# Early weight halves on VectorE, operand sums in a PSUM bank, a new order of memory attention: a two-block transformer forward pass on one core

## The chip, the cores and the metric

The kernel runs on one core of a Trainium2 chip. The metric is device time in microseconds of one execution, the median of several. The kernel before takes 3501.17 us (median of 3 runs, 3498.74 to 3503.02). Everything is float32; products are made on TensorE from two halves of each operand (below).

## What is computed

Two blocks are applied to x (512 tokens, width 1024). The first has two layers; each adds a mixer (layer 0: pooling and a gated recurrence, layer 1: banded attention), an attention over 256 memory tokens and a squared-ReLU MLP, with a norm ahead of and behind each:

```python
mem_n = rmsnorm(mem, mem_norm_gain)
for l in range(DEPTH):                     # 2 layers
    g = norm_gains[l]
    h = rmsnorm(x, g[0])
    y = even_mixer(h, ...) if l % 2 == 0 else odd_mixer(h, ...)
    x = x + rmsnorm(y, g[1])
    h = rmsnorm(x, g[2])
    x = x + rmsnorm(memory_cross_attention(h, mem_n, w_mem_q[l], w_mem_kv[l], w_mem_o[l]), g[3])
    h = rmsnorm(x, g[4])
    x = x + rmsnorm(squared_relu_mlp(h, w_ff1[l], w_ff2[l]), g[5])

def memory_cross_attention(h, mem_n, w_q, w_kv, w_o):      # 4 heads of 256
    q = (h @ w_q).reshape(B_, S_, MEM_HEADS, MEM_HEAD_DIM)
    kv = (mem_n @ w_kv).reshape(B_, M, 2, MEM_HEADS, MEM_HEAD_DIM)
    s = jnp.einsum('bshd,bmhd->bhsm', q, kv[:, :, 0]) * MEM_HEAD_DIM ** -0.5
    p = jax.nn.softmax(s, axis=-1)
    return jnp.einsum('bhsm,bmhd->bshd', p, kv[:, :, 1]).reshape(B_, S_, D_MODEL) @ w_o
```

The second block (a convolution and RWKV-7 mixer, then a product-key expert layer with 16384 experts) takes the rest of the time, from about 1700 us on. The change leaves its code alone.

## The kernel before, in words

**Program and queues.** Each engine has its own program, written by hand in one order: pe_program, dve_program, act_program, pool_program, sp_program. Engines meet through semaphores only (`wait_ge(at(...))`); an instruction that waits holds up everything behind it on its engine. The stages follow each other: memory (keys and values of both layers), even mixer, mem0, mlp0, odd mixer, mem1, mlp1, then the second block.

**Weights and halves.** Weights come in chunks of 1 MB through three raw buffers (`sp_loads`; the load of chunk r waits until both units of chunk r-3 are split). A chunk is two units of 128 x 1024 words. Each unit is split in two fp32r halves: ScalarE rounds it to the high half (`act_split`, L454), GpSimd subtracts to get the low half (`pool_split`, L462). The split tiles hold four units (slot u % 4), so unit u can be split only when the product that used unit u - 4 has ended (`unit_free`). A product is three matmuls per 128 rows of the contraction (`triple`, L476 to L478: high x high, low x high or high x low). Units are split AHEAD = 3 ahead of the product that reads them.

**Memory stage.** x and mem lie transposed (features on partitions, eight tiles c). ScalarE makes the high half of mem times gain (`act_operand`, L586) and its square (L587), VectorE the low half (`dve_operand_low`, L591) and the sum of the squares (`dve_operand_sum`, L598). TensorE sums them over partitions against a constant matrix (`pe_operand_sum`, L557), ScalarE takes the root (`act_root`, L572, L575), and the products are scaled by it as they leave PSUM. Keys: eight products per layer of 24 matmuls with 256 columns, one unit each (`pe_first` interleaves the first three over the eight tiles, `pe_product` makes the rest). Values: per layer four chunks, each read twice (`pe_token_product`, two token tiles tk), so a chunk's two units must both be ready at its start and come free only at its end; ScalarE scales the result (L822) between the splits of two units. Results go to DRAM by DMAs that GpSimd issues (`pool_key_out`, `pool_value_out`), three products late (KEY_LAG) so that they stand behind the splits, from rings of four buffers. The operand halves and squares of x for the even mixer are made in the same stage.

**Seams.** Between two branches (five places: even to mem0, mem0 to mlp0, mlp0 to odd, odd to mem1, mem1 to mlp1) `dve_add` on VectorE scales y by gain and root (L641), adds it to x (L648) and makes the low half (L591) of each of eight tiles; `act_add` on ScalarE first splits unit first + 3 of the next weights, then makes the high halves and squares. After the eight tiles VectorE adds the squares in y[:, 0, :] (L598, seven adds), while TensorE runs the first four products of the next stage (`pe_first` on three, then one more), and only then `pe_operand_sum`.

**Memory attention (mem0, mem1).** The order is the list of `mem_slots()`: each slot may hold a piece, which is one of the eight q products (24 matmuls with 512 columns) or a step of the first three o products, and an item m of 16 (head, token tile). TensorE does in a slot the piece, the score of item m, the transposes of item m - 3 (`pe_mem_spread`, L1373) and, where a head ended at item m - 5, its output products (`pe_mem_out`). VectorE scales q (L1450), makes its low half (L1454), the row extremes (L1464) and the normalised probabilities (L1470, L1472), and the low halves of the turned probabilities (L1495) and outputs (L1501). ScalarE makes the high halves and exponentials. Keys and values of the layer are split in halves at q piece 2 and 4 (`act_mem_halves`, `dve_mem_halves`, L1487).

PSUM has eight banks in one ring (`banks.take`, `banks.give`).

Of the kernel before, what the change touches and what calls it, by code (L numbers as in the profile page):

```python
# [9 lines left out]
F32 = mybir.dt.float32  # L10
# [4 lines left out]
P = 128  # L15
T = 512
D = 1024
CT = D // P
TT = T // P
M = 256  # L20
# [37 lines left out]
AHEAD = 3  # L58
# [198 lines left out]
def build(nc, dram, out, gate_table, early_table, memory_k, memory_v, x_tokens):  # L257
    ctx = ExitStack()
    with ctx:
# [154 lines left out]

        def split_ready(u):
            return at("split_high", u), at("split_low", u)
# [40 lines left out]
        def pool_split(upto):  # L457
            while state["low"] <= upto:
# [5 lines left out]
                state["low"] += 1  # L464

# [127 lines left out]

        def dve_operand_sum(stage, square):

            for c in range(1, CT):
                dve.wait_ge(at("operand_square", stage, c), at("operand_square", stage, 0) if c == 1 else dve.last)
                dve.do.tensor_tensor(square(0), square(0), square(c), ALU.add  # L598
                                     ).then_inc(*dve.sig("operand_sum", stage, c))
# [30 lines left out]
        def act_add(branch, stage, gain, first):  # L630
            act_split(first + AHEAD)
            for c in range(CT):
                act_operand(stage, c, x[:, c, :], gain, h_hi[:, c, :], y[:, c, :], x_ready(branch)(c))

        def dve_add(branch, gain, x_before, y_ready, stage=None, next_gain=None):
# [14 lines left out]
            if stage:  # L650
                dve_operand_sum(stage, lambda c: y[:, c, :])
# [93 lines left out]
        constant_names = ["columns"] + [k for k in CONSTANT_WIDTHS if k not in STAGE_CONSTANTS]  # L745
# [4 lines left out]
        def pool_inputs():  # L750
            for k in constant_names:
                pool.do.dma_start(columns if k == "columns" else const[k], dram[k]
                                  ).then_inc(*pool.land("constants_landed", k))
# [3 lines left out]
        def dve_inputs():  # L757
            dve.wait_ge(at("constants_landed", constant_names[-1]))
            for i, value in enumerate((NORM_EPS, LN_EPS, GN_EPS, 1.0)):
                dve.do.memset(scalars[:, i:i + 1], value).then_inc(*dve.sig("eps_set", i))  # L760
            dve_mod_gate()
# [64 lines left out]
        def pool_memory():  # L826

            pool_split(2 * W["keys", 0][0] + AHEAD)
            for l in range(2):
                for c in range(CT):  # L830
                    pool_split(2 * W["keys", l][0] + c + AHEAD)
                    if c >= KEY_LAG:
                        pool_key_out(l, c - KEY_LAG)
# [2556 lines left out]
```

## Time and profile before

| | |
|---|---|
| median of 3 runs | 3501.17 us |
| the profiled execution | 3501.14 us |
| its span in the profile | 3499.9 us |
| mean granted TensorE clock | 0.967 |

In the profile PE is TensorE, DVE VectorE, ACT ScalarE, POOL GpSimd, SP the queue that issues the weight loads; PEld is the loading of TensorE's stationary operand. L462 is line 462 of the kernel. A row of instructions names the engine, the line, the tiles written and read, and in brackets the idle time ahead of it with what ended it. Matmuls overlap: their records are longer than the distance between them, which is the rate.

### The profile page before, as it was taken

To read this page: it belongs to the slowest core of one execution; us is meant where nothing else is said; L and a number is where in the kernel's file an instruction comes from. 1 tells how busy PE (TensorE), PEld (TensorE's weight loads), DVE (VectorE), ACT (ScalarE), POOL (GpSimd) and SP (SyncE) were. 2 spreads that over 40 slices of the span, in tenths; PEclk is the share of its full clock that TensorE was granted. 3 is DMA by queue.
4 is the path that set the end of the run, shared out by engine and by line. 5 is a ranking of instruction groups with operands and counts; after the bars stand their busy time and mean duration, and the time that the engine had idled before them with its cause. 6 is when DMAs were issued, how large, how long until landed. Compare 5 with 4: busy or idle time off the path is not lost.

```text
span 3499.9 us, 48015 instructions
## 1 busy us (share of the span) xinstructions
PE 3248.4 (93%) x18529; PEld 2740.7 (78%) x18529; DVE 2253.0 (64%) x3780; ACT 1358.3 (39%) x2196; POOL 1715.9 (49%) x931
## 2 busy tenths in 40 slices
PE   6997888999899888999898898999999998999997
PEld 6886677888776677888576755799999998788886
DVE  4176646555544556553566646276998995888888
ACT  4444434222344434222253314333333674333332
POOL 6742323444332323444242202447888544888885
PEclk9998999999999999999898899999999999999999
DMA  5520212444322212443220011338899899999995
GB/s 193 183 76 25 87 58 92 137 139 139 108 91 67 84 45 88 145 144 109 69 85 31 3 37 60 120 141 292 295 325 326 266 311 304 372 357 350 354 356 219
DMA packets 304819, 584.76 MB, mean 167 GB/s; under 512 B 13520, under 2 KB 224464, under 8 KB 287312
## 3 DMA queue, kind: packets, MB, share of 16 engines
q1 hardware_dynamic: 252512, 373.32, 31.5%
q0 software_dynamic: 42576, 153.83, 12.2%
q10 hardware_dynamic: 9504, 54.53, 4.1%
q8 instruction: 149, 2.44, 0.3%
q14 instruction: 78, 0.64, 0.1%
HBM read 522.91 MB, written 58.72 MB: 166 GB/s over the span
## 4 chain that ended last, share of the span: by engine, by line
PE 64%; POOL 13%; DVE 9%; issue 8%; ACT 3%; DMA 1%; POOLq 0%; DVEq 0%; SPq 0%; ACTq 0%
PE bank L476 14%; PE bank L478 14%; PE bank L477 14%; POOL split_low L462 9%; PE twin L476 3%; PE twin L478 3%; PE twin L477 3%; PE bank L2854 2%; PE bank L557 2%; PE bank L2279 2%; POOL rows_arena L3220 2%; DVE branch L598 1%; POOL rows_h L3220 1%; POOL rows_near L3220 1%; DVE residual L648 1%
## 5 line engine op out<-in xcount | busy, mean ns | idle before, releaser
L462 POOL TENSOR_TENSOR split_low<-weights,split_high 128x1024 fp32r<-128x1024 f32 x554 | 1363.0, 2466 | 1494.7 <-ACT split_high L454 1490.9
L476 PE MATMUL bank<-normed_high,split_high 128*128 128x512 f32 (+1 forms) x2024 | 748.0, 370 | 34.6 <-issue 25.9
L477 PE MATMUL bank<-normed_low,split_high 128*128 128x512 f32 (+1 forms) x2024 | 736.7, 364 | 0.0
L478 PE MATMUL bank<-normed_high,split_low 128*128 128x512 f32 (+1 forms) x2024 | 736.5, 364 | 0.0
L454 ACT CAST split_high<-weights 128x1024 fp32r<-128x1024 f32 x554 | 571.4, 1046 | 359.8 <-PE bank L478 202.0
L476 PEld LDWEIGHTS bank<-normed_high,split_high 128*128 128x128 f32 x2024 | 384.1, 190 | 84.2 <-issue 37.0
L477 PEld LDWEIGHTS bank<-normed_low,split_high 128*128 128x128 f32 x2024 | 384.1, 190 | 41.6 <-issue 2.7
L478 PEld LDWEIGHTS bank<-normed_high,split_low 128*128 128x128 f32 x2024 | 383.3, 189 | 41.1
L476 PE MATMUL bank<-split_high,wide_hidden_high 128*128 128x512 f32 x768 | 300.2, 391 | 12.6 <-DVE wide_hidden_low L3076 7.4
L478 PE MATMUL bank<-split_high,wide_hidden_low 128*128 128x512 f32 x768 | 299.3, 390 | 0.0
L477 PE MATMUL bank<-split_low,wide_hidden_high 128*128 128x512 f32 x768 | 299.3, 390 | 0.0
L2749 ACT ACTIVATE branch<-bank 128x384 f32<-128x384 f32 x128 | 63.0, 492 | 309.0 <-PE bank L478 306.8
L476 PEld LDWEIGHTS bank<-split_high,wide_hidden_high 128*128 128x128 f32 x768 | 144.5, 188 | 45.9 <-issue 14.0
L1540 DVE SCALAR_TENSOR_TENSOR tmp<-weights,scalars,tmp 128x256 f32<-128x256 f32 x168 | 176.4, 1050 | 5.1
L3072 DVE TENSOR_TENSOR lates<-lates,gates 128x384 f32<-128x384 f32 x128 | 144.8, 1150 | 38.9 <-DMA gates<-gate_table 38.8
L478 PEld LDWEIGHTS bank<-split_high,wide_hidden_low 128*128 128x128 f32 x768 | 144.4, 188 | 30.1
L477 PEld LDWEIGHTS bank<-split_low,wide_hidden_high 128*128 128x128 f32 x768 | 144.6, 188 | 29.8
L2976 ACT CAST wide_hidden_high<-lates 128x384 fp32r<-128x384 f32 x128 | 65.6, 514 | 230.5 <-DVE lates L3072 166.6
L476 PE MATMUL bank<-hidden_high,split_high 128*128 128x512 f32 x384 | 150.7, 392 | 0.0
L3076 DVE TENSOR_TENSOR wide_hidden_low<-lates,wide_hidden_high 128x384 fp32r<-128x384 f32 x128 | 126.9, 991 | 36.0 <-ACT wide_hidden_high L2976 30.5
L478 PE MATMUL bank<-hidden_high,split_low 128*128 128x512 f32 x384 | 149.6, 390 | 0.0
L477 PE MATMUL bank<-hidden_low,split_high 128*128 128x512 f32 x384 | 149.4, 389 | 0.0
(636 smaller groups left out, 6265.3 us busy)
## 6 DMA issues: line engine op xcount, KB each, us to landing
weights<-in_w_ff SPq DMA_DIRECT2D x64, 1024.0 KB, 5.5
weights<-in_peer_u SPq DMA_DIRECT2D x64, 1024.0 KB, 7.4
weights<-in_peer_v SPq DMA_DIRECT2D x64, 1024.0 KB, 8.9
weights<-in_cond_w SPq DMA_DIRECT2D x24, 1024.0 KB, 5.3
early_table<-branch SPq DMA_DIRECT2D x128, 192.0 KB, 4.4
gate_table<-arena SPq DMA_DIRECT2D x12, 2048.0 KB, 9.8
lates<-early_table ACTq DMA_DIRECT2D x32, 768.0 KB, 9.6
gates<-gate_table ACTq DMA_DIRECT2D x32, 768.0 KB, 12.5
```

What stands on the lines that cost most here:

```text
L454: act.do.copy(unit_tiles(u)[0], raw_unit(u)).then_inc(*act.sig("split_high", u))
L462: pool.do.tensor_tensor(lo, raw_unit(u), hi.bitcast(F32), ALU.subtract).then_inc(*pool.sig("split_low", u))
L476: pe.do.matmul(o, ah, bh, start=first, stop=False)
L477: pe.do.matmul(o, ah, bl, start=False, stop=False)
L478: return pe.do.matmul(o, al, bh, start=False, stop=last)
L557: pe.do.matmul(banks.tile("sum", norm)[:, 0:n], matrix, rhs, start=i == 0, stop=i == count - 1).then_inc(*pe.sig("summed", norm, i))
L1540: dve.do.scalar_tensor_tensor(out=total, in0=wt[:, a, :], scalar=g_act[:, CT + a:CT + a + 1], in1=total, op0=ALU.mult, op1=ALU.add).then_i ...
L2279: last = pe.do.matmul(bank, raw_tile("conv", j)[:, at_tap * P:(at_tap + 1) * P], r_pad[:, c, tap:tap + T], start=tap == 0, stop=tap == CON ...
L2854: last = pe.do.matmul(bank[:, j * P:(j + 1) * P], hot[:, 0, t, :], hot[:, 1, t, :], start=True, stop=True)
L3072: dve.do.tensor_tensor(s, s, gates[n % 2][:, :, c, :], ALU.mult).then_inc(*dve.sig("gated_hidden", n, c))
L3076: dve.do.tensor_tensor(lo[:, c - 1, :], lates[n % 2][:, c - 1, :], hi[:, c - 1, :].bitcast(F32), ALU.subtract).then_inc(*dve.sig("hidden_l ...
L3220: pool.do.indirect_dma_start(out=v_rows[k % V_RING], out_offset=None, in_=dram["peer_v_rows"], in_offset=bass.IndirectOffsetOnAxis(ap=own_ ...
```

## The change

- The low halves of the first 34 units (the memory stage's 32 and the even mixer's first two) are made by VectorE (`dve_split`) and not by GpSimd, which in the memory stage now only issues DMAs, each as soon as its product is scaled (KEY_LAG is gone).
- The start waits for the columns alone, not for all constants; ScalarE loads its table first; the sigmoid of the modulation gate moves into the even mixer. The splits of the first units stand between the first operands in another order (FIRST_UNITS), and units 4 to 6 are split ahead of the root.
- VectorE makes the x operands' low halves between the values' splits, and adds their squares during layer 1's keys.
- At the five seams the running sum of the squares stands in a PSUM bank; each add reads one tile of y from SBUF. ScalarE splits unit first + 3 after the eight operands instead of ahead of them.
- In memory attention the keys' halves are made ahead of the root, and the pieces stand at other items: q4 to q7 at items 0, 3, 8, 11 (before 0, 2, 4, 6), o steps at 12, 13, 15, 16, 19, 20 (before 10, 11, 14, 15, 18, 19).

The diff, cut to its core:

```diff
+        EARLY = 2 * W["E", "f"][0] + 2
         def split_ready(u):
-            return at("split_high", u), at("split_low", u)
+            return at("split_high", u), at("early_low" if u < EARLY else "split_low", u)
+        def dve_split(upto):
+            while state["early"] <= min(upto, EARLY - 1):
+                u = state["early"]
+                hi, lo = unit_tiles(u)
+                dve.wait_ge(at("split_high", u), unit_free(u))
+                dve.do.tensor_tensor(lo, raw_unit(u), hi.bitcast(F32), ALU.subtract
+                                     ).then_inc(*dve.sig("early_low", u))
+                state["early"] += 1
+        def dve_running_sum(stage):
+            total = running_sum(stage)
+            for c in range(1, CT):
+                ...
+                dve.do.tensor_tensor(total if c < CT - 1 else y[:, 0, :], total, y[:, c, :], ALU.add
                                      ).then_inc(*dve.sig("operand_sum", stage, c))
         def act_add(branch, stage, gain, first):
+            act_split(first + FIRST - 1)
+            for c in range(CT):
+                act_operand(stage, c, x[:, c, :], gain, h_hi[:, c, :], y[:, c, :] if c else running_sum(stage),
+                            [x_ready(branch)(c), None if c else state["sum_empty", stage]])
             act_split(first + AHEAD)
-            for c in range(CT):
-                act_operand(stage, c, x[:, c, :], gain, h_hi[:, c, :], y[:, c, :], x_ready(branch)(c))
         def act_inputs():
-            act.wait_ge(at("constants_landed", constant_names[-1]), at("eps_set", 3))
-            act_mod_gate()
+            act.do.preload_act_table_set("natural_log_exp_and_others")
+            act.wait_ge(at("columns_landed"), at("eps_set", 3))
+        FIRST_UNITS = (-1, -1, 1, 1, 2, 2, 3, 3)
         def act_memory():
             for c in range(CT):
-                act_split(first + min(1 + c // 2, FIRST))
+                act_split(first + FIRST_UNITS[c])
                 ...
-            act_split(first + FIRST + 1)
-            act_logs()
+            act_split(first + 2 * FIRST)
             act_root("mem", 0, NORM_EPS, mem_root, M)
         def mem_slots():
-            slots += [(("q", 4), 0), (None, 1), (("q", 5), 2), (None, 3), (("q", 6), 4), (None, 5), (("q", 7), 6)]
-            return slots + [(("o",) if m > 9 and m % 4 in (2, 3) else None, m)
-                            for m in range(7, len(MEM_ITEMS) + OUT_LAG)]
+            pieces = {0: ("q", 4), 3: ("q", 5), 8: ("q", 6), 11: ("q", 7)}
+            pieces.update((m, ("o",)) for m in (12, 13, 15, 16, 19, 20))
+            return [(("q", c), None) for c in range(4)] + [(pieces.get(m), m) for m in range(len(MEM_ITEMS) + OUT_LAG)]
         def act_mem(l):
             act_split(q_unit + FIRST + AHEAD)
+            act_mem_halves("k", l, m_k, mk_high)
             act_root(st, 0, NORM_EPS, root)
         def dve_mem(l, before):
+            dve_mem_halves("k", l, m_k, mk_high, mk_low)
             for piece, m in mem_slots():
```

## Rows read from the trace of the kernel before

**Rows 1.** The page: the chain that ended last, by engine.

```profile
PE 64%; POOL 13%; DVE 9%; issue 8%; ACT 3%; DMA 1%; POOLq 0%; DVEq 0%; SPq 0%; ACTq 0%
```

**Rows 2.** Stretches: length, PE, PEld, DVE, ACT, POOL busy, clock, DMA share, GB/s.

```profile
64.00:87.00 23.00, 19.78 (x164) 19.43 (x163) 17.76 (x11) 9.40 (x13) 18.29 (x14) 1.00 0.53 173
87.00:110.00 23.00, 22.02 (x182) 21.67 (x181) 2.97 (x7) 7.33 (x7) 22.90 (x15) 1.00 0.70 225
```

**Rows 3.** DMA issues to 160 us: KB, median us to landing.

```profile
arena<-in_mem SPq DMA_DIRECT2D x1, 1024.0 KB, 5.6
columns<-in_columns POOLq DMA_DIRECT2D x1, 189.5 KB, 6.2
```

**Rows 4.** Timeline of the first 45 us: start, us, what, idle before.

```profile
10.07 1.28 ACT L1524 ACT_TABLE_LOAD   x1 [10.07 <-DVE scalars L760]
14.51 0.91 POOL L755 DMA_DIRECT2D residual<-in_x  x1 [9.79 <-DMA weights<-in_w_mem_kv]
15.52 9.31 POOL L462 TENSOR_TENSOR split_low<-weights,split_high 128x1024 fp32r<-128x1024 f32 x4
22.66 0.55 PE L476 MATMUL bank<-mem_high,split_high 128*128 128x256 f32 x1 [1.33 <-POOL split_low L462]
...
43.17 0.55 PE L476 MATMUL bank<-mem_high,split_high 128*128 128x256 f32 x1 [3.87 <-POOL split_low L462]
```

**Rows 5.** Timeline in the values of layer 0, and the even mixer's first sum.

```profile
60.55 0.47 ACT L822 ACTIVATE arena<-bank,token_root 128x256 f32<-128x256 f32 x1 [0.25 <-PE bank L478]
60.92 1.03 ACT L454 CAST split_high<-weights 128x1024 fp32r<-128x1024 f32 x1
63.11 0.35 PE L476 MATMUL bank<-split_high,mem_high 128*128 128x256 f32 x1 [2.60 <-POOL split_low L462]
68.39 14.00 DVE L598 TENSOR_TENSOR branch<-branch 128x512 f32<-128x512 f32 x7
70.63 0.56 POOL L852 DMA_DIRECT2D memory_v<-arena  x1
136.36 1.02 PE L557 MATMUL bank<-branch,const_mean 128*128 128x512 f32 x2
```

**Rows 6.** Forms on VectorE to 1400 us: count, busy, mean ns.

```profile
L598 DVE TENSOR_TENSOR branch<-branch 128x512 f32<-128x512 f32 x42 | 63.6, 1515 | 3.8
L1584 DVE TENSOR_TENSOR branch<-branch,bank 128x512 f32<-128x512 f32 x42 | 27.6, 681 | 35.1 <-PE bank L478 35.0
L1487 DVE TENSOR_TENSOR mem_k_low<-arena,mem_k_high 128x1024 fp32r<-128x1024 f32 x4 | 4.7, 1221 | 0.5 <-ACT mem_k_high L1426 0.5
```

**Rows 7.** VectorE writing PSUM, whole execution: count, busy, mean ns.

```profile
L3033 DVE SCALAR_TENSOR_TENSOR twin<-rows_arena,own_z,twin 128x1024 f32<-128x1024 f32 x55 | 70.8, 1287 | 10.4 <-DMA rows_arena<-in_peer_v_rows,own_expert 6.1 <-DVE twin L3033 0.5
```

**Rows 8.** Timeline of the seam into mem0.

```profile
390.46 2.70 POOL L462 TENSOR_TENSOR split_low<-weights,split_high 128x1024 fp32r<-128x1024 f32 x1 [4.91 <-ACT split_high L454]
390.87 2.84 DVE L641 SCALAR_TENSOR_TENSOR branch<-branch,columns,tmp 128x512 f32<-128x512 f32 x1
409.79 9.48 DVE L598 TENSOR_TENSOR branch<-branch 128x512 f32<-128x512 f32 x7
412.36 2.95 ACT L454 CAST split_high<-weights 128x1024 fp32r<-128x1024 f32 x3 [2.82 <-PE bank L478]
413.50 8.00 POOL L462 TENSOR_TENSOR split_low<-weights,split_high 128x1024 fp32r<-128x1024 f32 x3 [20.34 <-ACT split_high L454]
430.76 0.55 PE L476 MATMUL bank<-mem_k_high,mem_q_high 128*128 128x256 f32 x1 [4.78 <-issue]
```

**Rows 9.** Who waited for the adds of L598, whole execution: us, times.

```profile
  PE bank L557: 9.5, 3
  PE twin L557: 0.9, 2
```

**Rows 10.** TensorE's waits in mem0, 425 to 536 us: total, times, longest.

```profile
PE bank L476 <- DVE mem_turned_low L1495: 7.1, 3, 3.5
PE twin L476 <- DVE mem_turned_low L1495: 2.2, 1, 2.2
```

**Rows 11.** TensorE in a stretch of mem0: length, busy, granted clock, DMA.

```profile
480.00:490.00 10.00, 7.78 (x33) 0.83 0.00 0
```

More of the change, by code:

```diff
@@ L592, in dve_operand_low, with dve_operand_add, pe_sum_bank, running_sum @@
                                         op1=ALU.subtract).then_inc(*dve.sig("operand_low", stage, c))
+        def dve_operand_add(stage, square, c):
+            dve.wait_ge(at("operand_square", stage, c),
+                        at("operand_square", stage, 0) if c == 1 else at("operand_sum", stage, c - 1))
+            dve.do.tensor_tensor(square(0), square(0), square(c), ALU.add
+                                 ).then_inc(*dve.sig("operand_sum", stage, c))
         def dve_operand_sum(stage, square):
             for c in range(1, CT):
[L597 to L598 removed]
+                dve_operand_add(stage, square, c)
+        def pe_sum_bank(stage):
+            state["sum_empty", stage] = banks.take("running_sum", stage)[1]
+            banks.give(("running_sum", stage), ("operand_sum", stage, CT - 1))
+        def running_sum(stage):
+            return banks.tile("running_sum", stage)
+        def dve_running_sum(stage):
+            total = running_sum(stage)
+            for c in range(1, CT):
+                dve.wait_ge(at("operand_square", stage, c),
+                            at("operand_square", stage, 0) if c == 1 else at("operand_sum", stage, c - 1))
+                dve.do.tensor_tensor(total if c < CT - 1 else y[:, 0, :], total, y[:, c, :], ALU.add
                                      ).then_inc(*dve.sig("operand_sum", stage, c))
@@ L744, in build @@
         rings += [k_out, v_out]
-        constant_names = ["columns"] + [k for k in CONSTANT_WIDTHS if k not in STAGE_CONSTANTS]
+        constant_names = [k for k in CONSTANT_WIDTHS if k not in STAGE_CONSTANTS]
         def sp_inputs():
@@ L855, in dve_memory @@
         def dve_memory():
+            first = 2 * W["keys", 0][0]
+            square = lambda e: y[:, e, :]
             for c in range(CT):
+                dve_split(first + FIRST_UNITS[c])
                 dve_operand_low("mem", c, mem_raw[:, c, :], mem_gain, mem_hi[:, c, :], mem_lo[:, c, :],
@@ L859, in dve_memory @@
             dve_operand_sum("mem", lambda c: mem_square[:, c, :])
+            dve_split(first + 2 * FIRST)
             for l in range(2):
                 for c in range(CT):
+                    dve_split(2 * W["keys", l][0] + c + AHEAD)
                     s, empty = k_out.take(l, c)
@@ L866, in dve_memory @@
                     k_out.give((l, c), k_written(l, c))
+                    if l == 1 and c:
+                        dve_operand_add(EM, square, c)
                 if l == 0:
                     dve_token_root("mem", 2, 4)
-                    for e in range(CT):
-                        dve_operand_low(EM, e, x[:, e, :], gain_of(0, 0), h_hi[:, e, :], h_lo[:, e, :], at("x_landed"))
-                    dve_operand_sum(EM, lambda e: y[:, e, :])
+                for n, i in enumerate(W["values", l]):
+                    for tk in range(M // P):
+                        dve_split(2 * i + tk + AHEAD - 1)
+                        if l == 0:
+                            e = 2 * n + tk
+                            dve_operand_low(EM, e, x[:, e, :], gain_of(0, 0), h_hi[:, e, :], h_lo[:, e, :],
+                                            at("x_landed"))
         EM = "even"
@@ L3332, in write @@
                 ring.restart()
-            state.update(loaded=0, high=0, low=0, mod=None)
+            state.update(loaded=0, high=0, early=0, low=EARLY, mod=None)
             pe_program()
```

41 lines of the change are left out of this document (15 added, 26 removed).

## The prediction, made before the change was run

> **What bounds the kernel now.** The page's chain comes first: TensorE carries 64% of it, but GpSimd has 13% and VectorE 9% [rows 1]. Both are engines on which TensorE waits, so I looked for the stretches where they stand in the chain. They are three: the memory stage (22 to 136 us), the five seams, and the two memory attentions. The change edits just these; the second block, from 1700 us on, follows as it is.
>
> In the memory stage the windows show GpSimd full: 22.90 of 23.00 us busy in layer 1's keys, where a low half, its DMA issue and a key product take the same 2.9 us [rows 2]. In the values, where a chunk's units come free only at its end, TensorE waits for GpSimd: 2.60 us ahead of the second chunk [rows 5]; the reader sees 19.78 busy of 23 us in [rows 2], and 1.5 to 1.7 us more ahead of each later chunk. At a seam GpSimd and VectorE block each other: the adds take 9.48 us where GpSimd splits three units, and the second L641 takes 2.84 us beside the split of one [rows 8].
>
> **Part 1, the memory stage.** *Start.* ScalarE now starts at 10.07, after all constants and ahead of a table load of 1.28 us [rows 4]. After the change it needs mem and the columns, which land 5.6 and 6.2 us after their issue at 0.75 and 1.28 [rows 3], so it starts near 7.6. TensorE's steady start is bound by the third unit, in chunk 1, which landed just ahead of 14.51 [rows 4], at about 13.9. Now GpSimd makes four lows in a row from 15.52 (9.31 us) and the third is used at 22.66 [rows 4]. After: landed 13.9, ScalarE 1.03 [rows 5], VectorE's low 1.22, the nearest row being a difference of the same shape with both sources in SBUF [rows 6], and some 0.1: 16.2. Gain 6.4.
>
> *Units 4 to 6 ahead of the root.* The product of unit 5 starts at 43.17 after an idle of 3.87 [rows 4]; its matmuls then stand 0.21 us apart for 5 us and not 0.12, a loss of 2.3 more. After, the splits follow the first products directly, in 1.0 + 1.2 us under products of 2.9. I take back 0.8 for units 8 and 9, which stand on ScalarE behind six operand pairs of x (1.15 us each) and come late for the first values chunk. Gain 5.4.
>
> *Values.* Per chunk the chain is: first product 3.04 to its end, result scaled in 0.4, split 1.03 [rows 5], low 1.22 [rows 6], hand-overs 0.1: 5.8 us against 5.76 of matmuls (48 at 0.12). So 23.4 us for four chunks. Layer 0 takes 32.5 now (54.5 to 87.0): gain 9.1. Layer 1 takes 26.5 (110.0 to 136.4, [rows 5]): gain 3.1. Layer 1's keys stay at 23.0: TensorE is full there anyway.
>
> Sum of the stage 24.0; with a few tenths for chunk hand-overs **23.7**. VectorE has per unit 1.22 for the low half, 0.42 to scale a key or 0.75 for an x low: under 2.9. What hides the x adds (7 x 0.69) are layer 1's keys; without that cover they would cost up to 5. The bound on the other side: should VectorE's lows be held up as the adds beside GpSimd were (2.0 us each, [rows 5], 14.00 for seven), each of eight chunks is 0.8 longer, and up to 1.5 if 2.7 as at the seams: gain 12 to 23.7. I take the upper end, since GpSimd has no tensor work left there. On the queues: GpSimd's DMAs now wait for nothing but their product, ScalarE loses a table load, and the gate's sigmoid and product (0.2 us each and one table load, which the key sigmoids needed anyway) stand in the even mixer beside five us of matmuls per product: nothing. The weight loads must come each 5.8 us; in [rows 2] 225 GB/s were moved, and 182 are needed.
>
> The Trainium skill, SBUF — State Buffer, section "Who interferes with whom", has a rule against this part: descriptors of DMAs that GpSimd issues cannot be written while VectorE holds the shared ports in a two-port mode, which would delay the key and value writes. In this trace an issue takes 0.56 us in the midst of VectorE's two-source adds [rows 5], the form of the lows, so the trace does not bear it out for them, and the sum would not move.
>
> **Part 2, the seams (five).** *Start.* L641 takes 2.84 and not 0.75 since GpSimd splits unit first + 3 [rows 8]; all five seams show 2.83 or 2.84. Behind it the chain is VectorE alone, so 1.9 us come back each: 9.5. What is late next is that unit: ScalarE splits it after its eighth operand, at 407.7 to 408.7 by the new clock of the seam, GpSimd until 411.2; the product that reads it starts at 411.5. The cover is 0.3 us; were it gone, up to 0.5 a seam is lost (GpSimd at 2.7). Nothing taken.
>
> *Adds.* An add with one source in SBUF and one in PSUM takes 0.681 in 42 cases beside the same splits, where the all-SBUF one takes 1.515 [rows 6]. No row adds in place in PSUM at this size; the nearest writes PSUM from one PSUM and one SBUF source, 1.287 for 1024 elements, so 0.65 to 0.70 for 512 [rows 7]. Seven adds then end about 5.6 us after the last low half, ahead of the end of the fourth product, so TensorE's wait goes: 9.5 at the MLP and odd seams, 0.9 at the two others [rows 9]: 10.4. If the adds were still blocked, 0 of it. The same skill section says that VectorE with two SBUF inputs contends with GpSimd's reads and with one does not: by that rule the sum is the 10.4 that the rows give. Taking a bank adds no wait: it was last used eight allocations earlier.
>
> Sum **19.9** (9.5 if the adds stay blocked).
>
> **Part 3, memory attention (two).** Root times come with part 2. From there, now: three q tiles at 1.98 us each, then the keys' lows, so the first score stands at 430.76 after 4.78 idle [rows 8]. After, the score needs only q tile 1's low half, at root + 3.9: 1.0 idle. The keys' lows go under the wait for the sum; GpSimd splits at that time (413.50 for 8.00, [rows 8]) and may hold each of the two to 2.7; they end near 419 with the root at 419.6, so this cover is thin, and costs at most 1. But taking q6 and q7 out of the first items lays the softmax open: item 0's row extreme comes on VectorE behind q3, q4 and the values' lows, at root + 13.3; TensorE has done q4, q5 and four scores by 12, and until 21 it has 4 us of small work, so it idles about 5, in place of 3.5 ahead of head 0's outputs. Later q6, q7 and the o steps stand between turn and output of each head, and what TensorE waits there (the rest of 7.1 + 2.2 of [rows 10], and 0.6 for one item, so 6.5) goes but for 1. Idle: 14.8 now, 7 after. With it the clock: 0.83 in ten us with 7.78 busy [rows 11], and over 430 to 490 us the shortfalls from 1.00 add up to 6.8 us; I halve that, since the early idle remains. 7.8 + 3.2 = 11 a stage, **22** for both. Bounds: 2 x 4 if the exposed softmax takes all the rest, 2 x 17 if all idle and slow stretches but 5 us go.
>
> **Sum.** 23.7 + 19.9 + 22 = 65.6 us. The profiled execution took 3501.1 with a span of 3499.9, the same as the median of the runs. Predicted 3501.1 - 65.6 = **3435.5**.
>
> **Rivals.**
> - *VectorE's low halves are late in the memory stage* (hand-over through ScalarE's result, ports, or the weight loads). For: the values' chain of 5.8 has no slack. Against: VectorE's row. Part 1 gives 12: 3447.
> - *The new order of memory attention only moves the wait to its first items.* For: 13 us from root to the first extreme. Against: the later waits are surely covered. Part 3 gives 8: 3449. With the first rival: 3461.
> - *The adds in PSUM stay blocked*, the change doesn't do what it says: 3446.
> - *Slower: TensorE is granted less.* The mean granted clock is 0.967. Busy for 3248 us, TensorE loses about 32 us per 0.01. If denser work lowered the grant, 0.02 less eats the whole gain, and 0.025 gives 3516. Place: everywhere. Against: the rows with idle TensorE have the low clock (0.83, [rows 11]), the full ones have 1.00 [rows 2].
> - *More than forecast*: memory attention at its upper bound: 3424.
>
> **How the numbers follow.** Forecast (within 7 us) 0.45; late low halves 0.13; memory attention little 0.15; adds blocked 0.05; two of these together 0.06; more 0.14; slower 0.01; none of it 0.01. The range 3415 to 3461 leaves out less than 2 in 10 with both bounds. Within 0.2% (7 us, about what a measurement can tell from no change) 0.01, slower 0.01, faster 0.98.
>
> **What would show it.** The sum of the even mixer (L557, now 136.36) near 113; GpSimd without tensor work before 115; values chunks 5.8 us apart. At the seams no L641 over 0.8 and the new adds at 0.7; TensorE's wait ahead of L557 under 0.5. In memory attention, the first score 4 us after the root, no wait for L1495 over 1 us, and an idle of about 5 around items 0 to 4. The forecast is wrong if the stage's end is after 118, if the fourth product of a seam waits for unit first + 3, or if the clock in the full stretches is under 1.00.

## The result, and the profile after

The changed kernel takes 3450.94 us (median of 4 runs, 3448.0 to 3452.21) beside 3502.1 for the kernel before on the same chip (3498.74 to 3504.43): ratio 0.9857, interval 0.9838 to 0.9877. The forecast was 3435.5 with a range to 3461: the sign and the range hold, and 15.4 us of the forecast gain did not come.

The page of the changed kernel, beside the chain of [rows 1]: its span, busy times, mean clock row and chain.

```profile
span 3450.9 us, 48001 instructions
PE 3237.6 (94%) x18529; PEld 2733.9 (79%) x18529; DVE 2239.0 (65%) x3814; ACT 1358.0 (39%) x2195; POOL 1631.9 (47%) x897
...
PEclk9998999999999999999898999999999999999999
...
PE 67%; POOL 12%; DVE 8%; issue 7%; ACT 4%; DMA 1%; POOLq 0%; DVEq 0%; SPq 0%; ACTq 0%
```

GpSimd's share of the chain only fell from 13% to 12%, since most of it lies in the second block; the shares alone don't tell where 49 us went. For that I cut both spans at twelve landmarks that both kernels have: TensorE's operand sum of each stage (L557 before, L568 after) and the first residual product of each seam on VectorE (L641 before, L675 after). Lengths of the pieces in us, with the forecast's steps beside them:

| piece | before | after | gain | forecast |
|---|---|---|---|---|
| memory stage, to 136.36 / 113.09 | 136.36 | 113.09 | 23.3 | 23.7 |
| even mixer | 253.12 | 249.95 | 3.2 | 0 |
| five seams | 156.04 | 137.76 | 18.3 | 19.9 |
| memory attention, layers 0 and 1 | 118.17, 117.76 | 119.95, 119.50 | -1.8, -1.7 | 11, 11 |
| MLPs, to the next seam | 340.35, 338.32 | 338.65, 336.62 | 1.7, 1.7 | 0 |
| odd mixer | 243.39 | 240.29 | 3.1 | 0 |
| second block | 1796.39 | 1795.09 | 1.3 | 0 |

So two of the three parts came as forecast, the third gave back 3.5 where 22 were expected, and 11 us came that no step had. Each column is one profiled execution, so a small difference says little: over the kernels of the experiments that share the code of a piece, the memory stage ends at 112.4 to 113.8 (nine of them), the memory attentions with the new order take 118.7 to 120.3 and 117.9 to 119.5 (six), and the second block 1790.6 to 1796.8 (all). The 1.3 of the second block is within that.

**Memory stage.** TensorE's waits of the first 60 us, after ([rows 4, 5] hold those of before): start, length, what, idle ahead with its releaser.

```profile
13.30 0.55 PE L487 MATMUL twin<-mem_high,split_high 128*128 128x256 f32 x1 [13.30 <-ACT mem_high L597]
...
14.44 0.55 PE L487 MATMUL twin<-mem_high,split_high 128*128 128x256 f32 x1 [0.15 <-DVE split_low L473]
...
16.61 0.55 PE L487 MATMUL bank<-mem_high,split_high 128*128 128x256 f32 x1 [1.19 <-DVE split_low L473]
...
42.13 0.36 PE L487 MATMUL bank<-split_high,mem_high 128*128 128x256 f32 x1 [0.16 <-DVE split_low L473]
...
60.38 0.35 PE L487 MATMUL twin<-split_high,mem_high 128*128 128x256 f32 x1 [0.34 <-DVE split_low L473]
```

The third unit is used at 16.61 where it was 22.66, the 3.87 ahead of unit 5 [rows 4] is gone, and the values' waits of 2.60 [rows 5] are 0.34 at most. Stretches of the same length as those of [rows 2], same columns:

```profile
42.00:65.00 23.00, 22.53 (x182) 22.09 (x183) 13.93 (x17) 11.83 (x17) 4.88 (x9) 1.00 0.77 244
65.00:88.00 23.00, 23.00 (x194) 23.00 (x193) 18.25 (x24) 9.71 (x10) 4.34 (x8) 1.00 0.76 243
```

GpSimd is down from 22.90 of 23 us to 4.34, and all of that is DMA issue.

**Seams.** VectorE at the seam into mem0, after, beside [rows 8], and GpSimd's splits there:

```profile
364.44 0.74 DVE L675 SCALAR_TENSOR_TENSOR branch<-branch,columns,tmp 128x512 f32<-128x512 f32 x1
...
381.55 2.30 DVE L630 TENSOR_TENSOR bank<-bank,branch 128x512 f32<-128x512 f32 x3
...
382.32 10.44 POOL L464 TENSOR_TENSOR split_low<-weights,split_high 128x1024 fp32r<-128x1024 f32 x4 [23.20 <-ACT split_high L456]
...
384.31 2.31 DVE L630 TENSOR_TENSOR bank<-bank,branch 128x512 f32<-128x512 f32 x3 [0.46 <-DVE bank L630]
...
384.86 0.47 PE L487 MATMUL twin<-normed_high,split_high 128*128 128x512 f32 x1 [0.54 <-POOL split_low L464]
```

The second L675 takes 0.74 where it took 2.84, and three adds take 2.30 right beside GpSimd's four splits. All seven are done at 387.41, 5.8 us behind the last low half (5.6 was forecast) and ahead of TensorE's sum at 390.42, which now follows its product without a wait. In [rows 8] the seven took 9.48.

**Memory attention.** TensorE's waits in mem0 after, 390 to 510 us (total, times, longest), to be read beside [rows 10]:

```profile
PE bank L487 <- DVE mem_turned_low L1529: 8.4, 4, 2.6
PE twin L1409 <- DVE arena L1506: 6.3, 3, 3.1
PE bank L487 <- DVE mem_q_low L1490: 0.6, 1, 0.6
```

Two stretches of it, beside [rows 11]:

```profile
410.00:420.00 10.00, 4.86 (x22) 4.00 (x21) 7.04 (x16) 4.43 (x12) 2.35 (x1) 0.52 0.00 0
420.00:430.00 10.00, 10.00 (x41) 8.23 (x40) 2.14 (x5) 2.68 (x5) 2.39 (x1) 0.80 0.00 0
```

The idle is 15.3 us, where it was 14.8 before and 7 were forecast, and the wait between turn and output (L1529), which was to go but for 1, is 8.4 (9.3 before). The granted clock falls to 0.52 in the middle of it.

### The profile page after: what moved, and what is told of

It is laid out like the page before. It is cut to its first block, busy times and chain, and to the rows that moved or that the text cites. A ratio compares the mean times of both kernels' runs of the same rounds, so it can differ in the third digit from the quotient of the medians.

```text
span 3450.9 us, 48001 instructions
## 1 busy us (share of the span) xinstructions
PE 3237.6 (94%) x18529; PEld 2733.9 (79%) x18529; DVE 2239.0 (65%) x3814; ACT 1358.0 (39%) x2195; POOL 1631.9 (47%) x897
## 4 chain that ended last, share of the span: by engine, by line
PE 67%; POOL 12%; DVE 8%; issue 7%; ACT 4%; DMA 1%; POOLq 0%; DVEq 0%; SPq 0%; ACTq 0%
PE bank L487 15%; PE bank L489 15%; PE bank L488 15%; POOL split_low L464 8%; PE twin L487 3%; PE twin L489 3%; PE twin L488 3%; PE bank L2890 3%; PE bank L568 2%; PE bank L2315 2%; POOL rows_arena L3256 1%; POOL rows_h L3256 1%; POOL rows_near L3256 1%; PE bank L2122 1%; DVE residual L682 1%
## 5 line engine op out<-in xcount | busy, mean ns | idle before, releaser
L464 POOL TENSOR_TENSOR split_low<-weights,split_high 128x1024 fp32r<-128x1024 f32 x520 | 1276.4, 2461 | 1451.7 <-ACT split_high L456 1448.2
L1574 DVE SCALAR_TENSOR_TENSOR tmp<-weights,scalars,tmp 128x256 f32<-128x256 f32 x168 | 159.8, 951 | 5.1
L1669 ACT ACTIVATE arena<-arena 128x512 f32<-128x512 f32 x64 | 40.5, 633 | 257.8 <-DVE arena L1690 257.8
```

Source lines behind the costliest of these rows:

```text
L464: pool.do.tensor_tensor(lo, raw_unit(u), hi.bitcast(F32), ALU.subtract).then_inc(*pool.sig("split_low", u))
L1574: dve.do.scalar_tensor_tensor(out=total, in0=wt[:, a, :], scalar=g_act[:, CT + a:CT + a + 1], in1=total, op0=ALU.mult, op1=ALU.add).then_i ...
```

## The step that failed, found in the code

Why do q6, q7 and the o steps not stand between turn and output? The prediction took `MEM_LAG, OUT_LAG = 3, 5` (L1312 before, L1348 after) for what it says. But the odd mixer's `TURN_LAG, OUT_LAG = 2, 3` (L1687 before, L1722 after) sets the same name in the same scope ahead of the writing of the programs. So in both kernels a head's outputs are asked for three items after its probabilities, in the same slot as its last transposes. Between them stand no pieces in either order. The account of the kernel before, which has the output products at item m - 5, is wrong by the same reading: they stand at item m - 3. The list of slots ends two items earlier too, at 18, so the o steps named for items 19 (both kernels) and 20 (the changed one) were made behind the last item. That can be tested.

## Experiments

Each is the changed kernel with the edit shown; ratios are to the kernel before on the same chip, and the stage lengths are those of memory attention in layers 0 and 1, cut as in the table. The kernel before took 3499.5 us beside experiments 1 to 4, 3493.6 beside 5 to 8, 3502.1 beside 9 to 11 and 3498.0 beside 12, so times of different groups are compared by ratio or by the lengths of pieces.

**1. The lag that the text says.**

```diff
-        TURN_LAG, OUT_LAG = 2, 3
+        TURN_LAG, ODD_OUT_LAG = 2, 3
```
(with ODD_OUT_LAG in the four uses of the odd mixer)

> The changed kernel with memory attention's own output lag: the outputs of a head five items behind the scores, as the order of the pieces is written for, and not three (a constant of the odd mixer with the same name sets it to three). Theory of the lag: q6 and q7 (items 8 and 11) and the o steps then stand between turn and output, the 8.4 us of waits for the turned low halves in mem0 fall under 1.5, the low clock behind them goes, the stage from its sum to the next seam falls from 120 to about 110.5 us, the time by about 19 to 3432. Rival, VectorE's queue bounds the stage: it keeps its softmax work, the waits only move to the scores or transposes, the stage stays at 117 or more and the time within 6 us of 3451.

Measured: 3436.77 us, ratio 0.9825 (0.9804 to 0.9845); stages 109.35 and 111.03. The one name is worth 10.6 and 8.5 us. TensorE's waits in mem0 in this kernel:

```profile
PE twin L1409 <- DVE arena L1506: 6.3, 2, 3.5
PE bank L487 <- DVE mem_turned_low L1529: 2.5, 1, 2.5
PE twin L487 <- DVE mem_turned_low L1529: 0.6, 1, 0.6
```

The waits for L1529 fall from 8.4 to 3.1, as the prediction had it of the change; those for the first probabilities (L1506) stay.

**2. The pieces at their old items.**

```diff
-            pieces = {0: ("q", 4), 3: ("q", 5), 8: ("q", 6), 11: ("q", 7)}
-            pieces.update((m, ("o",)) for m in (12, 13, 15, 16, 19, 20))
+            pieces = {0: ("q", 4), 2: ("q", 5), 4: ("q", 6), 6: ("q", 7)}
+            pieces.update((m, ("o",)) for m in (10, 11, 14, 15, 18, 19))
```

> The changed kernel with the pieces of memory attention at the items of before (q4 to q7 at 0, 2, 4, 6, o steps at 10, 11, 14, 15, 18, 19), lag three as it runs. Theory of the lag: the new positions cost more than they bring while the lag is three, since q6 and q7 no longer cover the softmax of the first items (6.3 us of waits for the probabilities in the trace of after); the stage falls from 120 to about 114 us, the time by about 11 to 3440. Rival, the keys' halves ahead of the root are what costs (VectorE held for 6.5 us beside GpSimd): the stage stays near 119 and the time near 3449.

Measured: 3441.35 us, 0.9836 (0.9816 to 0.9856); stages 112.61 and 113.28. With the lag as it is, the new order costs 7.3 and 6.2 us. Most of it is not idle time: that is 13.5 us in mem0 here and 15.3 in the changed kernel. The same matmuls take longer at a lower clock. The stage in layer 0, changed kernel first, then this one:

```profile
390.42:510.37 119.95, 103.15 (x471) 84.25 (x469) 55.48 (x98) 43.24 (x82) 32.15 (x13) 0.91 0.19 62
```

```profile
394.63:507.24 112.61, 97.73 (x471) 80.24 (x469) 57.15 (x98) 43.21 (x82) 32.17 (x13) 0.98 0.20 66
```

**3. Both.**

> The piece positions of before together with the lag of five, the fourth cell beside the changed kernel, the lag alone and the positions alone. Theory of the lag: head 0's outputs have only two small items between turn and output, so some 1.5 to 2 us of wait remain there, heads 1 to 3 are covered by o steps; the stage about 108 us, the time near 3428. Rival, VectorE's queue bounds the stage: as with the positions alone.

Measured: 3424.31 us, 0.9792 (0.9770 to 0.9813); stages 105.90 and 105.03. The waits in mem0:

```profile
PE twin L1409 <- DVE mem_turned_low L1529: 3.4, 1, 3.4
PE twin L1409 <- DVE arena L1506: 2.9, 1, 2.9
PE bank L487 <- DVE mem_q_low L1490: 0.6, 1, 0.6
```

Three waits are left of eight, 6.9 us of 15.3. Even at lag 5 the new order is 3.5 and 6.0 us worse than the old one: with q6 and q7 at later items the softmax of the first ones lies open (6.3 us behind L1506 in experiment 1, 2.9 here), which is what the rival of the first items said. In layer 1 the idle differs by 2.6 us only (8.9 and 6.3), and the rest of the 6.0 is the clock (0.95 and 0.98 over the stage).

**4. An order between the two, at lag 5.** q4 to q6 at items 0, 2, 4, q7 at 7, o steps at 11, 12, 15, 16, 19, 20.

> Lag five with q4 to q6 at items 0, 2, 4 (where they cover the first softmax), q7 at 7 (between turn and output of head 0) and the o steps at 11, 12, 15, 16, 19, 20. Theory of the lag: all four outputs covered and the first items filled, the stage about 106 us, the time near 3424, the fastest of the four orders. Rival, VectorE's queue bounds the stage: no faster than the positions of before with either lag.

Measured: 3424.82 us, 0.9793 (0.9772 to 0.9814); stages 106.44 and 105.58. The same as experiment 3 within what a measurement tells; that it would be the fastest was wrong.

**5. Unit first + 3 split ahead of the operands again.**

```diff
-            act_split(first + FIRST - 1)
+            act_split(first + AHEAD)
             for c in range(CT):
```

> The changed kernel with ScalarE's split of unit first + 3 ahead of the eight operands of a seam again. Theory of the shared port (GpSimd's low half holds VectorE's two-source instruction): the second L675 of all five seams takes 2.8 again and each seam is 1.9 us longer, the time about 9 us more than the changed kernel, 3460. Rival, the stall belongs to something else at the seam's start: 3451.

Measured: 3461.11 us, 0.9908 (0.9888 to 0.9929). VectorE and GpSimd at the seam into mem0:

```profile
363.33 2.83 DVE L675 SCALAR_TENSOR_TENSOR branch<-branch,columns,tmp 128x512 f32<-128x512 f32 x1
362.91 2.70 POOL L464 TENSOR_TENSOR split_low<-weights,split_high 128x1024 fp32r<-128x1024 f32 x1 [4.90 <-ACT split_high L456]
```

The stall is back at its old price, 2.09 longer than 0.74. All five seams show it. They are 1.78, 0.59, 1.83, 1.57 and 1.14 us longer than after the change, 6.9 in sum where the prediction had 9.5 for it: three by nearly its 1.9. Why the two seams into an MLP lose less I did not settle; the same rows stand in them. (The 0.59 is measured against a seam that took 27.89 in the changed kernel and 27.4 in most others; against those it is 1.1.)

**6. The adds with both sources in SBUF again.**

```diff
-            total = running_sum(stage)
+            total = y[:, 0, :]
```
(and the same for ScalarE's first square)

> The changed kernel with the seams' running sums in y[:, 0, :] in SBUF again (the bank is taken but not used). Theory of the shared port: the adds beside GpSimd's four splits take 2.7 each again, now for more of them, since unit first + 3 is split there too; seven adds take 14 or more. The MLP and odd seams lose 3.1 us of wait and some of the 1.7 us that a low clock costs behind it, and up to 3 more for the fourth split, the memory seams 1 to 3: 16 to 24 us more than the changed kernel, 3467 to 3475. Rival, the adds are hidden by the fourth product as their length was cut by the earlier start: 3453.

Measured: 3481.76 us, 0.9968 (0.9953 to 0.9982), more than any case expected. The adds (durations in ns) and who waited for them:

```profile
L630 DVE TENSOR_TENSOR branch<-branch x35: 683/2641/2930, 383.0 to 1347.0; 128x512 f32<-128x512 f32 x35
...
  PE bank L568: 14.2, 3
  PE twin L568: 9.6, 2
```

TensorE at the sum, in the timeline:

```profile
396.81 1.19 PE L568 MATMUL twin<-branch,const_mean 128*128 128x512 f32 x1 [4.82 <-DVE branch L630]
```

Now all five seams wait 4.7 to 4.8 us, where before it was 9.5 in three and 0.9 in two [rows 9]. The reason is the other edit of the change: with unit first + 3 split behind the operands, GpSimd has four splits beside the adds, not three, and they begin 0.8 us behind the first add (383.76 and 382.99), where it was 3.7 [rows 8]; the adds take 13.2 us. So the two edits of the seam are not independent, and an estimate of one alone from the trace of before (10.4) is too low once the other is in. And the pieces behind the seams grow too: the MLPs to 340.40 and 339.62 and the odd mixer to 242.81, that is 1.8, 3.0 and 2.5 us, while nothing in them is changed. The seams' 24.5 and these 7.3 are the 30.9 us by which the span is longer, the other pieces making up -0.9.

**7. The keys' halves after the root again.**

```diff
-            act_mem_halves("k", l, m_k, mk_high)
             act_root(st, 0, NORM_EPS, root)
...
+                    if c == 2:
+                        act_mem_halves("k", l, m_k, mk_high)
```
(the same on VectorE)

> The changed kernel with the keys' halves at q piece 2 again, behind the root. If the halves ahead of the root are worth what the trace of before showed (4.8 us of wait ahead of the first score, now 0.6), each memory stage is 4 to 5 us longer and the time 9 more, 3460. Rival, they only move a wait (VectorE held 6.5 us beside GpSimd ahead of the root, and the softmax behind it has slack since the first items are idle anyway): within 3 us of 3451.

Measured: 3453.87 us, 0.9883 (0.9863 to 0.9903), stages 120.62 and 122.16. The first score waits 4.8 us again, but with the new order the items behind it wait 4.1 less (in mem0, 2.2 us for the probabilities and not 6.3): 0.7 and 2.7 us lost. The 0.7 is within what profiles of the same code differ by, and of the 2.7 only 0.8 is idle time.

**8. The early low halves by GpSimd again** (`EARLY = 0`, with GpSimd's program of the memory stage as before).

> The changed kernel with all low halves of the weights made by GpSimd again (the memory stage's GpSimd program of before; the earlier start, the order of the first splits and the rest of the change stay). Theory that VectorE's low halves are worth the gain of the stage: third unit used near 22, values chunks 7.5 us apart in layer 0, the even mixer's sum near 130 and not 113, the time 16 to 20 more, 3468. Rival, the gain came from the start, the units ahead of the root and the x operands' order: under 8 more.

Measured: 3474.71 us, 0.9941 (0.9919 to 0.9962). The even mixer's sum stands at 135.53, and the third unit at 22.66, to the hundredth as in [rows 4]:

```profile
22.66 0.55 PE L487 MATMUL bank<-mem_high,split_high 128*128 128x256 f32 x1 [1.32 <-POOL split_low L464]
...
60.44 0.35 PE L487 MATMUL bank<-split_high,mem_high 128*128 128x256 f32 x1 [2.30 <-POOL split_low L464]
```

22.4 of the 23.3 us of the memory stage hang on this one edit; the start and the order of the units, which this kernel keeps, give 0.8 without it, less than the spread of the stage (1.5).

**9. Units 4 to 6 split after the root.**

```diff
-            act_split(first + 2 * FIRST)
+            act_split(first + FIRST + 1)
             act_root("mem", 0, NORM_EPS, mem_root, M)
```

> The changed kernel, but in the memory stage units 4 to 6 are split after the root of mem, not ahead of it; all else as changed. Theory (the prediction's term of 5.4 us): the second key product waits for its units again. ScalarE can split unit 5 only after the root, TensorE idles 3 to 4 us ahead of it and its next matmuls run at a lower clock; sum of the even mixer 4 to 6 us later than 113.09, so 117 to 119, time about 3456. Rival (VectorE makes a low half in 1.2 us where GpSimd took 2.3, so the order of the splits no longer matters): sum at 113 to 115, time 3451 to 3453.

Measured: 3454.82 us, 0.9877 (0.9850 to 0.9905); the sum at 115.59, 2.5 later than in the changed kernel. Between the two cases: TensorE waits for the unit, but 2.71 us and without the slow matmuls behind it that made the prediction's other 2.3.

```profile
35.59 0.36 PE L487 MATMUL bank<-mem_high,split_high 128*128 128x256 f32 x1 [2.71 <-DVE split_low L473]
```

**10. Both units of a values chunk split ahead of its first result**, with the order and lag of experiment 3.

```diff
-                        act_split(2 * i + tk + AHEAD - 1)
+                        act_split(2 * i + AHEAD)
```

> As the kernel with the old piece order and lag 5 in memory attention (3424.3), and in the memory stage's values both units of a chunk are split ahead of the chunk's first result, where now one stands ahead of it and one behind. Theory (the values chunks stand 6.0 to 6.15 us apart since the chain product, result, split, low half has no slack against 5.8 of matmuls): with two splits ahead, chunks are 5.8 apart, eight chunks give 2 to 2.5 us, sum of the even mixer near 111, time near 3422. Rival (the 0.2 to 0.3 us per chunk are TensorE's own, such as its queue, or a unit's buffers only come free when the chunk ends): sum at 113, time 3424 as before.

Measured: the sum at 110.75, 2.3 us earlier than in experiment 3 (113.06): the chunks' missing 0.2 to 0.3 us were the chain through result and split, as the theory says. The time is 3427.03 us, 0.9789 (0.9761 to 0.9817), by the ratio the same as experiment 3 (0.9792): in the profiled execution layer 1's memory attention took 107.73 where the same code took 105.03. Both had the same two large waits there (2.9 and 3.4), and this one 0.9 more ahead of the first score; the rest is the clock. The same ten us (from 1170), experiment 3 first, then this one:

```profile
1170.00:1180.00 10.00, 7.13 (x39) 6.03 (x38) 8.79 (x11) 4.46 (x9) 3.94 (x2) 1.00 0.31 105
```

```profile
1170.00:1180.00 10.00, 7.12 (x33) 5.97 (x32) 8.22 (x11) 5.25 (x10) 4.45 (x2) 0.85 0.32 105
```

**11. ScalarE's start waits for all constants.**

> The changed kernel, but ScalarE's start waits for all constants again, not for the columns alone. Theory (the prediction's start term of 6.4 us is mostly VectorE's low halves, since the third unit is bound by chunk 1, which lands near 13.9): ScalarE's first operand at 8.8 to 9, sum of the even mixer at most 1 us later (113 to 114), time 3451 to 3452, no change that can be measured. Rival (ScalarE's queue of operands and splits sets the third unit, so its start counts in full): sum 1.2 to 2.4 us later, 114.3 to 115.5, time about 3453.

Measured: 3453.82 us, 0.9874 (0.9846 to 0.9901); first operand at 9.99 (7.64 in the changed kernel), yet the sum only 0.6 later, at 113.71. Of ScalarE's 2.4 us, 1.7 went into its wait for chunk 0:

```profile
10.85 1.99 ACT L456 CAST split_high<-weights 128x1024 fp32r<-128x1024 f32 x2 [1.70 <-DMA weights<-in_w_mem_kv]
```

That line is the changed kernel's. The third unit is used 0.55 later (17.16 and 16.61), which bears the 0.6 out, though the sum alone would not: nine kernels with one program of the stage spread over 1.5. The rest of the prediction's start term is VectorE's low halves.

**12. Memory attention wholly as before**: experiments 2 and 7 together.

> The changed kernel with memory attention wholly as before: pieces at their old items (lag 3) and the keys' halves made at q piece 2, not ahead of the root. With the pieces alone put back the stages took 112.6 and 113.3 us, and before they took 118.2 and 117.8; so 4.5 to 5.6 us a stage come from something else in the change. Theory A (it is the keys' halves, since the first score waited 4.78 us for them): stages at 117 to 118, time near 3450. Theory B (with the halves late and all other things changed the new order lost only 0.7 and 2.7 us; the rest is TensorE's clock, 0.83 in four stretches before, which is not tied to the halves): stages at 113.5 to 116, time 3443 to 3447.

Measured: 3445.8 us, 0.9853 (0.9831 to 0.9875); stages 116.16 and 118.66. The expected times don't decide, since they depend on the kernel that one adds to: stages of 117.5 give 3450 from experiment 2 and 3446 from the changed kernel. The stage lengths do, in sum: 234.8 is theory A's 234 to 236 and not theory B's 227 to 232. In the old order the keys' halves ahead of the root are thus worth 3.6 and 5.4 us (against experiment 2), where the new order lets through only 0.7 and 2.7. But only 1.3 and 1.9 of this is idle time; the rest is the clock, and two stages with the same idle time here differ by 2.5 us. TensorE in the memory attentions, layer 0 and layer 1, from its sum to the next seam:

| kernel | length | idle | granted clock |
|---|---|---|---|
| before | 118.17, 117.76 | 14.7, 14.8 | 0.94, 0.94 |
| changed | 119.95, 119.50 | 15.3, 15.1 | 0.91, 0.93 |
| 1 (lag 5) | 109.35, 111.03 | 10.0, 8.9 | 0.98, 0.95 |
| 2 (old order) | 112.61, 113.28 | 13.5, 12.8 | 0.98, 0.97 |
| 3 (both) | 105.90, 105.03 | 6.9, 6.3 | 0.98, 0.98 |
| 12 (as before) | 116.16, 118.66 | 14.8, 14.7 | 0.96, 0.93 |

So in this stage the clock weighs as much as the waits: from the changed kernel to experiment 2 the idle time of layer 0 falls by 1.8 us and the length by 7.3. In sum the stages here take 4.6 us less than the changed kernel's 239.5; all six profiles with the new order and the halves ahead of the root at lag 3 stand at 237.9 to 239.8, above the 234.8 here and the 235.9 before. So part 3 as built loses 2 to 5 us to leaving memory attention alone. The ratios of the two kernels (0.9853 and 0.9857) are too close to show it.

## Why the prediction was right, and where it failed

**Part 1 (23.7, measured 23.3).** Right in its sum. The start was forecast at 16.2 for the third unit and came at 16.61; the values' chain was forecast at 5.8 a chunk and came at 5.96, 5.96 and 6.33, the difference being the wait in the chain that experiment 10 takes out. The low half itself was 1.22, the row it was taken from. But how the sum is split was only half right: the start term belongs to VectorE (experiment 11: 0.6 for the early start), and the 5.4 for units 4 to 6 is 2.5 once VectorE makes the lows (experiment 9), since a late unit then comes in 2.7 us and not 3.9. The terms were worked out each against the kernel before, and overlap. The rival of late low halves did not come; nor did the issue of GpSimd's DMAs suffer beside VectorE's two-source operations:

```profile
L875 POOL DMA_DIRECT2D memory_v<-arena x16 | 8.7, 542 | 37.7 <-ACT arena L856 37.7
L871 POOL DMA_DIRECT2D memory_k<-arena x16 | 8.7, 543 | 44.2 <-DVE arena L892 44.2
```

**Part 2 (19.9, measured 18.3).** Right, with both its mechanisms shown by experiments 5 and 6. The seams became shorter by 2.56, 4.12, 4.52, 2.23 and 4.85 us. The wait of the fourth product for unit first + 3, one of the prediction's own signs of being wrong, came in three seams, at 0.5 to 0.7 us (its cover was called thin and put at nothing). The missing 1.6 is not it, though: those three gave 9.6 where 9.9 were forecast. Most of it lies in the seams mem0 to mlp0 and mlp0 to odd (4.12 and 4.52, forecast 5.0 each), where no such wait stands but the clock over the seam is 0.88 and not 0.94. That the adds stay blocked was refuted: 0.70 each, 35 of them, beside the splits.

**Part 3 (22, measured -3.5).** The failed step is the sentence "Later q6, q7 and the o steps stand between turn and output of each head, and what TensorE waits there goes but for 1." It was read from a line of the code that another line overrides, and the trace of before could have told: the waits for L1495 in [rows 10] stand directly behind the transposes, at lag 3. With the lag really 5 (experiment 1) the gain is 8.8 + 6.7 = 15.5. Of what is then missing of 22, 4.9 is idle time (10.0 and 8.9, forecast 7 each): 3.1 and 3.2 behind L1529 where 1 was forecast, and 6.3 and 4.8 behind L1506 where the exposed softmax had 5, which was thus nearly right. The rest is the clock: the forecast added 3.2 a stage for it, experiment 1 gives about 4.1 and 0.9, and the changed kernel lost instead (0.91 and 0.93 over the stages, 0.94 before). The rival of the first items, 8 for both stages, has the waits of the first items right (6.3 us behind L1506, 0.6 there before), but the later ones did not go, as it too took for sure. Experiment 3, with the old order, gives 12.3 + 12.7 = 25.0. The cover of the keys' low halves was real but thin, as said; in mem0 they took 6.52 for the two beside GpSimd (2.7 each was forecast) and ended at 393.85, where ScalarE's root work had begun at 391.48 and taken 1.3: a microsecond late. The first score waits 0.58 where 1.0 was forecast and 4.78 had been.

**What came beside it (11.0, forecast 0).** The MLPs' 1.7 each: TensorE is at 1.00 where it was not, though the code there is the same. The first 30 us behind the seam's sum, before and then after:

```profile
569.60:600.00 30.40, 30.40 (x127) 24.67 (x128) 19.63 (x30) 16.00 (x23) 9.29 (x4) 0.94 0.35 118
```

```profile
538.30:568.30 30.00, 30.00 (x134) 24.51 (x133) 22.77 (x31) 16.02 (x23) 10.27 (x5) 1.00 0.41 139
```

0.06 of 30 us is 1.8 us. Experiment 6, where the seams wait again and nothing else is changed, brings it back (1.8 and 3.0), so this is shown: a wait of 3 to 5 us ahead of a full stretch costs about 2 us (1.7 to 3.0) more than its length. (Behind the seams into memory attention, where TensorE soon waits again, nothing of the kind was seen.) The odd mixer gains 1.6 to 3.1 in the same way (240.3, or 241.4 to 241.8, in the twelve kernels with the short wait, 242.8 and 243.4 in the two with the long one). The even mixer's 3.2 is another matter. Its code is the same in the changed kernel and all twelve others, and its length was 248.9 to 250.8 us in nine of these thirteen and 252.8 to 253.5 in four; before, it was 253.1. So the 3.2 can't be called a gain of the change, nor can the second block's 1.3. In one of the long ones (experiment 11) the clock is low where in the changed kernel it is full, in the ten us that begin 191.3 us behind the sum in both:

```profile
305.00:315.00 10.00, 6.91 (x26) 5.43 (x27) 6.18 (x11) 2.56 (x4) 0.00 (x0) 0.72 0.00 0
```

```profile
304.40:314.40 10.00, 7.98 (x50) 6.91 (x49) 4.62 (x9) 1.94 (x3) 0.00 (x0) 1.00 0.01 2
```

**The sum.** By the spans 65.6 were forecast and 49.0 came: part 1 -0.4, part 2 -1.6, part 3 -25.5, the clock and the rest +11.0. That the range held is luck in part: without the 11.0 the time would be 3462, past the range's end at 3461. Of these, 5 to 6.5 (the MLPs and the odd mixer) follow from the shorter waits of part 2, and the rest can't be told from chance. By its number the result is that of the rival "memory attention little" (3449, given 0.15), not of the forecast (0.45), and part 3 came lower still than that rival's 8. The rival "granted less" was not seen in any kernel: the mean clock of the profiled executions was 0.969 to 0.976, but for the 0.967 of experiment 6, and 0.967 before.

## What to carry to other kernels

Before costing a new order of work, find in the trace of the old one the distance between the two instructions that the order is to separate, and check that it is the one the code seems to name: one overridden constant cost 19 of the 25.5 us that part 3 fell short by, and undoing it, with the old order kept, gives 3424.3 us, 0.9792 of the kernel before. Terms that a forecast adds up should be worked out one on top of the other, not each against the kernel before: the order of the units fell from 5.4 to 2.5 and the adds rose from 10.4 to 24.5 once their neighbours were in. And a wait ahead of a full stretch is dearer than it looks: price it with the clock rows behind it.

## What the runs showed of the hardware

Where VectorE and GpSimd both read two tiles in SBUF, a VectorE instruction took 1.6 to 2.1 us longer here than alone, whatever its length (0.68 to 1.22 us). The keys' low halves, the same instruction with GpSimd splitting beside it (changed kernel) and with GpSimd idle (experiment 7):

```profile
L1521 DVE TENSOR_TENSOR mem_k_low<-arena,mem_k_high 128x1024 fp32r<-128x1024 f32 x4 | 11.1, 2806 | 0.0
```

```profile
L1523 DVE TENSOR_TENSOR mem_k_low<-arena,mem_k_high x4: 1218/1222/1224, 399.9 to 1183.8; 128x1024 fp32r<-128x1024 f32 x4
```

For 512 elements it is 0.68 against a median of 2.64 (experiment 6), so a small instruction pays as much as a large one. It waits for one of GpSimd's: the four slow adds of experiment 6's first seam each end 0.55 us behind the end of a split (386.70 behind 386.15, 389.52 behind 388.97). With one of its two sources in PSUM the add stays at 0.69 to 0.70, in place, in all 35 cases. This agrees with the Trainium skill, SBUF — State Buffer, section "Who interferes with whom", which says that VectorE with two SBUF inputs contends with a GpSimd instruction that reads SBUF and with one such input does not.

The granted clock of a stretch is not fixed by its code: the even mixer had 0.72 or 1.00 over the same ten us in kernels that don't differ there, with lengths of 248.9 to 253.5 in all, and layer 1's memory attention 105.0 or 107.7 us. A clock lost and won this way is a large part of what the orders of memory attention differ by: the same 471 matmuls of a stage were busy for 103.15 us in the changed kernel and 97.73 in experiment 2. A difference of this size between two profiled executions proves nothing about an edit elsewhere; lengths between landmarks close to the edit do.
